# Identity and x loaded in parts, the angles' sine moved to chunk 7, and block A's last down product moved ahead of block B's last gate and up

## The reference, cut to what matters

```python
def first_block(x, ...):
    for l in range(DEPTH):                      # DEPTH = 2
        f = swiglu(rms_norm(x, ffn1_pre_g[l]), ffn1_w_gu[l], ffn1_w_down[l])
        x = x + 0.5 * rms_norm(f, ffn1_post_g[l])
        m = hybrid_mixer(rms_norm(x, mix_pre_g[l]), ...)
        x = x + rms_norm(m, mix_post_g[l])
        f = swiglu(rms_norm(x, ffn2_pre_g[l]), ffn2_w_gu[l], ffn2_w_down[l])
        x = x + 0.5 * rms_norm(f, ffn2_post_g[l])

def second_block(x, positions, ...):            # the same shape without the norms behind
    cos_r, sin_r = rope_tables(positions, 128); cos_m, sin_m = rope_tables(positions, 32)
    for l in range(DEPTH):
        x = x + 0.5 * swiglu_ffn(rms_norm_2(x, ffn1_norm[l]), ...)
        x = x + (retention and latent attention of rms_norm_2(x, mix_norm[l])) @ w_o[l]
        x = x + 0.5 * swiglu_ffn(rms_norm_2(x, ffn2_norm[l]), ...)
```

## Time and profile before

| | |
|---|---|
| Median of 3 runs | 2165.37 us (2163.66 to 2166.07) |
| Profiled execution | 2167.78 us, of which the span of the profile is 2166.5 us |
| TensorE busy | 1980.8 us, 91% of the span |
| VectorE, ScalarE, GpSimd busy | 1179.8, 1020.3 and 123.1 us |
| Mean granted TensorE clock | 0.967 of full speed |
| Share of the chain that ended last | PE 80%, DVE 9%, ACT 6%, issue 3%, POOL 3% |
| Data moved | 348.08 MB, mean 161 GB/s |

### The profile page before, as it was taken

How to read it: one execution, slowest core, us unless ns; L and a number is a source line. 1 busy time by engine, 2 the same in 40 slices (tenths; PEclk the granted TensorE clock), 3 DMA queues, 4 the chain that set the end, 5 groups by cost and what they waited for, 6 DMA issues and landing times.

```text
span 2166.5 us, 23846 instructions
## 1 busy us (share of the span) xinstructions
PE 1980.8 (91%) x9304; PEld 1645.9 (76%) x9304; DVE 1179.8 (54%) x1695; ACT 1020.3 (47%) x1675; POOL 123.1 (6%) x183
## 2 busy tenths in 40 slices
PE   2999887999899987999999996889999999688999
PEld 1888786888788786788778875778877887577887
DVE  2555666555655576555564455555555456555554
ACT  3444564444544475444454453544445444354443
POOL 4000021000000012000000012000000001200000
PEclk9999998999999997999999998999999999889999
DMA  4655323655555433455555542345545554233553
GB/s 150 209 189 191 117 98 126 206 191 196 173 191 198 149 127 118 139 192 194 174 174 198 178 134 97 117 133 191 198 158 182 192 175 137 95 117 128 193 193 108
DMA packets 95904, 348.08 MB, mean 161 GB/s; under 512 B 10800, under 2 KB 10800, under 8 KB 95408
## 3 DMA queue, kind: packets, MB, share of 16 engines
q1 hardware_dynamic: 94032, 339.57, 47.4%
q10 hardware_dynamic: 1728, 6.99, 0.9%
q0 software_dynamic: 32, 0.00, 0.0%
HBM read 345.47 MB, written 1.05 MB: 160 GB/s over the span
## 4 chain that ended last, share of the span: by engine, by line
PE 80%; DVE 9%; ACT 6%; issue 3%; POOL 3%; DMA 0%; ACTq 0%; POOLq 0%; DVEq 0%
PE ps_gu L362 16%; PE ps_gu L364 16%; PE ps_gu L363 16%; PE ps_acc L362 9%; PE ps_acc L363 9%; PE ps_acc L364 9%; DVE sb_wl L1184 4%; PE ps_tr L417 2%; ACT sb_wh L805 1%; POOL sb_scratch L1648 1%; ACT sb_xh L834 1%; PE ps_acc L381 1%; ACT sb_scratch L826 1%; DVE sb_scratch L1299 1%; PE ps_acc L542 0%
## 5 line engine op out<-in xcount | busy, mean ns | idle before, releaser
L1184 DVE TENSOR_TENSOR sb_wl<-sb_raw,sb_wh 128x1024 fp32r<-128x1024 f32 (+2 forms) x648 | 769.7, 1220 | 289.9 <-ACT sb_wh L805 281.8
L362 PE MATMUL ps_gu<-sb_wh,sb_xh 128*128 128x512 f32 (+2 forms) x1632 | 667.0, 409 | 93.4 <-DVE sb_xl L1231 43.9
L805 ACT ACTIVATE sb_wh<-sb_raw 128x1024 fp32r<-128x1024 f32 (+2 forms) x648 | 658.1, 1053 | 193.2 <-PE ps_acc L364 136.0
L364 PE MATMUL ps_gu<-sb_wh,sb_xl 128*128 128x512 f32 (+2 forms) x1632 | 645.4, 395 | 0.0
L363 PE MATMUL ps_gu<-sb_wl,sb_xh 128*128 128x512 f32 (+2 forms) x1632 | 644.1, 395 | 0.0
L362 PEld LDWEIGHTS ps_gu<-sb_wh,sb_xh 128*128 128x128 f32 x1632 | 313.4, 192 | 160.8 <-DVE sb_xl L1231 43.0
L364 PEld LDWEIGHTS ps_gu<-sb_wh,sb_xl 128*128 128x128 f32 x1632 | 313.1, 192 | 66.5
L363 PEld LDWEIGHTS ps_gu<-sb_wl,sb_xh 128*128 128x128 f32 x1632 | 314.8, 193 | 57.6
L362 PE MATMUL ps_acc<-sb_wh,sb_fr 128*128 128x512 f32 (+1 forms) x768 | 301.3, 392 | 8.9 <-DVE sb_fr L1269 8.9
L363 PE MATMUL ps_acc<-sb_wl,sb_fr 128*128 128x512 f32 (+1 forms) x768 | 299.7, 390 | 0.0
L364 PE MATMUL ps_acc<-sb_wh,sb_fr 128*128 128x512 f32 (+1 forms) x768 | 299.3, 390 | 0.0
(11 more groups left out here) (264 smaller groups left out, 1322.2 us busy)
## 6 DMA issues: line engine op xcount, KB each, us to landing
sb_raw<-stream SPq DMA_DIRECT2D x628, 512.0 KB, 4.5
sb_raw<-stream SPq DMA_DIRECT2D x8, 416.0 KB, 3.8
sb_raw<-stream SPq DMA_DIRECT2D x8, 390.0 KB, 3.7
sb_gpost<-post_gains ACTq DMA_DIRECT2D x6, 512.0 KB, 3.4
sb_params<-params ACTq DMA_DIRECT2D x2, 1128.5 KB, 5.8
sb_raw<-stream SPq DMA_DIRECT2D x4, 384.0 KB, 4.1
sb_x<-x SPq DMA_DIRECT2D x1, 1024.0 KB, 7.2
out<-sb_x SPq DMA_DIRECT2D x4, 256.0 KB, 2.2
```

Source lines behind the costliest of these rows:

```text
L362: pe.matmul(out, xh, wh, start=start, stop=False)
L364: return pe.matmul(out, xl, wh, start=False, stop=stop)
L805: go(m.wh[:, u % RING, 0:widths[u]], m.raw[:, u % RAW, 0:widths[u]], ACT.Copy).then_inc(*s.high_done.up())
L1184: tt(m.wl[:, u % RING, 0:w], m.raw[:, u % RAW, 0:w], m.wh[:, u % RING, 0:w].bitcast(F32), ALU.subtract).then_inc(*s.low_done.up())
```

## The change

1. The constants are loaded in two parts, the identity (128 columns) first, then the gains, then the rest. x is loaded by block, B's half behind the first two units of the stream. TensorE waits for the identity and block A's half, and for B's half at `turn_x(0, 1)`.
2. ScalarE and VectorE split one unit, then work on block A's x, then one unit, and then two. The sine and its negation move to the end of chunk 7 of stage 0. GpSimd's program keeps `angles()` as its first work.
3. In the last chunk of every feed-forward stage, the turn of A's hidden values and A's down product come directly behind B's down product of the chunk before, ahead of B's gate and up. The next stage's `turn_x(e, 0)` is placed within B's gate and up: behind its last quarter ahead of a mixer, behind its third quarter ahead of a feed-forward stage with a norm behind, and behind its second in the others. B's last turn and down product (`rest` on TensorE, called `finish` in the next stage) run in the middle of the next stage's A products, and `turn_x(e, 1)` comes behind those.
4. ScalarE and VectorE follow: two units of the next stage are split before the boundary; at the boundary `first` (B's silu or hidden values; two splits after a mixer) and `second` (the split of B's hidden values and two units; two splits after a mixer) stand at new places. For a feed-forward stage `first` comes behind `x_high` and `x_low` of block A, whatever stage went before.
5. The mean behind the sum is computed as soon as both squares are there, ahead of the second product with the gain. GpSimd's roots come in the order of the blocks.

```diff
             elif e:
                 pe.wait_ge(*s.x_ready[t].at(2 * (e - 1) + half + 1))
+            elif t:
+                pe.wait_ge(s.x_b_loaded, 16)
...
-    def ffn(f, e):
+    def ffn(f, e, finish):
...
-        turn_x(e, 0)
-        for j in range(CHUNKS):
-            if j == 0:
-                gate_up(j, 0, lambda: turn_x(e, 1), 2)
-            else:
+        last = CHUNKS - 1
+
+        def rest():
+            turn_hidden(last, 1)
+            down(last, 1)
+
+        if finish:
+            gate_up(0, 0, finish)
+            turn_x(e, 1)
+        else:
+            turn_x(e, 0)
+            gate_up(0, 0, lambda: turn_x(e, 1), 2)
+        for j in range(last):
+            if j:
                 gate_up(j, 0, lambda: turn_hidden(j - 1, 1))
                 down(j - 1, 1)
             gate_up(j, 1, lambda: turn_hidden(j, 0))
             down(j, 0)
-        turn_hidden(CHUNKS - 1, 1)
-        down(CHUNKS - 1, 1)
+        gate_up(last, 0, lambda: turn_hidden(last - 1, 1))
+        down(last - 1, 1)
+        turn_hidden(last, 0)
+        down(last, 0)
+        if e + 1 == len(STAGES):
+            gate_up(last, 1)
+        elif STAGES[e + 1][0] != "ffn":
+            gate_up(last, 1, lambda: turn_x(e + 1, 0), 3)
+        else:
+            gate_up(last, 1, lambda: turn_x(e + 1, 0), 2 if e + 1 <= POSTS else 1)
+        return rest
...
-        turn_x(e, 0)
-        chunk(e, 0, zdt, ZDT_W, m.gu[0][:, 0:ZDT_W], True, lambda: turn_x(e, 1), 2).then_inc(
-            *done("zdt0", l))
+        chunk(e, 0, zdt, ZDT_W, m.gu[0][:, 0:ZDT_W], True, finish).then_inc(*done("zdt0", l))
+        turn_x(e, 1)
...
-    pe.wait_ge(s.const_loaded, 16)
+    pe.wait_ge(s.ident_loaded, 16)
+    finish = None
     for e, (kind, n) in enumerate(STAGES):
-        {"ffn": ffn, "mix1": mix1, "mix2": mix2}[kind](n, e)
+        finish = {"ffn": ffn, "mix1": mix1, "mix2": mix2}[kind](n, e, finish)
+    finish()
...
+        post, mixer = 1 <= e <= POSTS, STAGES[e][0] != "ffn"
         for t in range(2):
             if post:
                 post_squares(e, t)
-            if t == 0:
-                between()
+            if e == 0 and t == 1:
+                act.wait_ge(s.x_b_loaded, 16)
             if mixer:
                 x_squares(e, t)
+            else:
                 x_high(e, t)
-            elif e < len(STAGES):
-                if t == 1:
-                    x_squares(e, 0)
+            if t == 0:
+                first()
+            if mixer:
                 x_high(e, t)
-                if t == 1:
-                    x_squares(e, 1)
+            else:
+                x_squares(e, t)
             if t == 0:
-                after()
+                second()
...
-        for j in range(CHUNKS):
+        last = CHUNKS - 1
+        for j in range(last):
             split(2)
             if j == 0:
                 load_ahead()
@@ -886,7 +912,21 @@
             hidden_high(j, 0)
             split(2)
             silu(j, 1)
-        return lambda: hidden_high(CHUNKS - 1, 1), lambda: None
+            if e == 0 and j == 7:
+                act.wait_ge(*s.angles.at(1))
+                for i in range(2):
+                    a = go(m.trig[:, i, :, :], m.trig[:, i, :, :], ACT.Sin)
+                a.then_inc(*s.trig.up())
+        split(2)
+        hidden_high(last - 1, 1)
+        silu(last, 0)
+        hidden_high(last, 0)
+        split(2)
+
+        def rest():
+            hidden_high(last, 1)
+            split(2)
+        return lambda: silu(last, 1), rest
...
-    act.dma_start(m.const[:, :], aps["const"]).then_inc(s.const_loaded, 16)
+    act.dma_start(m.const[:, 0:P], aps["const"][:, 0:P]).then_inc(s.ident_loaded, 16)
     act.dma_start(m.gpre[:, :, :], aps["pre_gains"]).then_inc(s.gains_loaded, 16)
+    act.dma_start(m.const[:, P:CONST_COLS], aps["const"][:, P:CONST_COLS]).then_inc(s.const_loaded, 16)
...
-    act.wait_ge(*s.angles.at(1))
-    for i in range(2):
-        a = go(m.trig[:, i, :, :], m.trig[:, i, :, :], ACT.Sin)
-    a.then_inc(*s.trig.up())
     act.wait_ge(s.x_loaded, 16)
     act.wait_ge(s.gains_loaded, 16)
-    split(4)
-    between = after = lambda: None
+    split(1)
+    first, second = lambda: split(1), lambda: split(2)
...
-    def update_post(e, t, between):
+    def update_post(e, t):
         vec.wait_ge(s.post_gain_loaded, 16 * e)
         post_scale(e, t, 0)
-        between()
-        post_scale(e, t, 1).then_inc(*s.post_scaled[t].up())
+        vec.wait_ge(*s.post_squared[t].at(2 * e))
         ts(m.pm[:, t:t + 1], m.pss[:, t, 0:1], m.pss[:, t, 1:2], EPS * (4 if HALF_STEP[e] else 1), ALU.add,
            ALU.add).then_inc(*s.post_mean[t].up())
+        post_scale(e, t, 1).then_inc(*s.post_scaled[t].up())
...
+        post, stage = 1 <= e <= POSTS, STAGES[e][0] if e < len(STAGES) else None
         for t in range(2):
-            first = between if t == 0 else nothing
             if post:
-                update_post(e, t, first)
+                update_post(e, t)
             elif e:
                 update(e, t)
-                first()
-            if mixer:
+            if stage == "ffn":
+                x_low(e, t)
+            elif stage:
                 x_mean(e, t)
                 normed(e, t)
+            if t == 0:
+                first()
+            if stage == "ffn":
+                x_mean(e, t)
+            elif stage:
                 x_low(e, t)
-            elif e < len(STAGES):
-                if t == 1:
-                    x_mean(e, 0)
-                x_low(e, t)
-                if t == 1:
-                    x_mean(e, 1)
             if t == 0:
-                after()
+                second()
...
+            if e == 0 and j == 7:
+                vec.wait_ge(*s.trig.at(1))
+                ts(m.trig[:, 2, :, :], m.trig[:, 1, :, :], -1.0, None, ALU.mult).then_inc(*s.trig.up())
+        split(2)
+        hidden_low(last - 1, 1)
+        hidden(last, 0)
+        hidden_low(last, 0)
+        split(2)
+
+        def rest():
+            hidden_low(last, 1)
+            split(2)
+        return lambda: hidden(last, 1), rest
...
-            if STAGES[e][0] != "ffn":
-                x_rms(e, t)
-            elif t == 1:
-                x_rms(e, 0)
-        if STAGES[e][0] == "ffn":
-            x_rms(e, 1)
+            x_rms(e, t)
...
-    sp.dma_start(m.x[:, :, :], aps["x"]).then_inc(s.x_loaded, 16)
+    sp.dma_start(m.x[:, 0, :], aps["x"][:, 0, :]).then_inc(s.x_loaded, 16)
     for u in range(UNITS):
+        if u == 2:
+            sp.dma_start(m.x[:, 1, :], aps["x"][:, 1, :]).then_inc(s.x_b_loaded, 16)
...
```

More of the change, by code:

```diff
@@ L491, in mix1 @@
         tile(1, tiles + 1, m.gu[1][:, 0:T])
+        pe.wait_ge(s.const_loaded, 16)
         pe.wait_ge(*V.at("ad", l))
@@ L609, in part @@
         def part(t, u0, name, width=512, first=False, midway=None):
-            p = chunk(e, t, u0, width, m.gu[t][:, 0:width], first, midway, 2)
+            p = chunk(e, t, u0, width, m.gu[t][:, 0:width], first, midway)
             p.then_inc(*done(f"{name}{t}", turn))
@@ L691, in retained @@
             p.then_inc(*done(f"y{t}", turn))
-        turn_x(e, 0)
-        part(0, lat, "lat", LAT_W, True, lambda: turn_x(e, 1))
+        part(0, lat, "lat", LAT_W, True, finish)
+        turn_x(e, 1)
         part(1, lat, "lat", LAT_W, True)
@@ L836, in x_high, with boundary @@
             a.then_inc(*s.x_high[t].up())
-    def boundary(e, between, after):
-        post, mixer = 1 <= e <= POSTS, e < len(STAGES) and STAGES[e][0] != "ffn"
+    def boundary(e, first, second):
+        post, mixer = 1 <= e <= POSTS, STAGES[e][0] != "ffn"
         for t in range(2):
@@ L1147, in mix2 @@
         return lambda: split(2), lambda: split(2)
-    act.dma_start(m.const[:, :], aps["const"]).then_inc(s.const_loaded, 16)
+    act.dma_start(m.const[:, 0:P], aps["const"][:, 0:P]).then_inc(s.ident_loaded, 16)
     act.dma_start(m.gpre[:, :, :], aps["pre_gains"]).then_inc(s.gains_loaded, 16)
+    act.dma_start(m.const[:, P:CONST_COLS], aps["const"][:, P:CONST_COLS]).then_inc(s.const_loaded, 16)
     table(SILU)
-    act.wait_ge(*s.angles.at(1))
-    for i in range(2):
-        a = go(m.trig[:, i, :, :], m.trig[:, i, :, :], ACT.Sin)
-    a.then_inc(*s.trig.up())
     act.wait_ge(s.x_loaded, 16)
     act.wait_ge(s.gains_loaded, 16)
-    split(4)
-    between = after = lambda: None
+    split(1)
+    first, second = lambda: split(1), lambda: split(2)
     for e, (kind, n) in enumerate(STAGES):
-        boundary(e, between, after)
-        between, after = {"ffn": ffn, "mix1": mix1, "mix2": mix2}[kind](n, e)
-        assert at_unit[0] == min(FIRST_UNIT[e + 1] + 4 * (kind == "ffn"), UNITS), (e, kind, at_unit[0])
-    between()
+        boundary(e, first, second)
+        first, second = {"ffn": ffn, "mix1": mix1, "mix2": mix2}[kind](n, e)
+        assert at_unit[0] == min(FIRST_UNIT[e + 1] + 2 * (kind == "ffn"), UNITS), (e, kind, at_unit[0])
+    first()
+    second()
 def vector_program(nc, m, s, m1, m2):
```

(15 more changed lines are left out.)

9 lines of the change are left out of this document (5 added, 4 removed).

## The result

The changed kernel takes 2187.47 us (median of 4 runs, 2184.18 to 2189.09), the kernel before 2165.72 beside it (4 runs, 2163.66 to 2168.34): ratio 1.0098, 95% interval 1.008 to 1.0115, so slower by 17 to 25 us. I had forecast slower, at 2172.9 and not above 2182. The profiled execution took 2189.09 us (span 2187.5, for 2166.5 before), and TensorE's mean granted clock was 0.956 for 0.967.

What follows compares the result with a forecast made beforehand. TensorE works 91% of the span, so only its waits at the start and eleven boundaries count: -11.7 + 11.2 + 3.8 - 3.4 + 2.0 + 3.2 + 2.4 = +7.5, 2172.9 us by the median; 8-in-10 range 2161 to 2182.

Steps and rivals of the forecast that it cites:

- The start: Stage 0: turn of A's hidden values at 40.5 for 53.70, less 1.5 for a slow stretch; gain 11.7, bounds 9.5 to 17.6.
- Rival 3: Start: the angles aren't on the path, so the start follows the first product, 29 us earlier; 2155.6, chance 0.06.
- The clock: Boundaries: slow stretches cost 2.1 each at stages 1, 4 and 1.1 each at 7, 10; -3.2 at 3, 6, 9; sum +3.2.
- stages 1 and 4: Feed-forward to mixer: B's first product after 27.5 us for 29.2, -1.7 each, before the clock's 2.1 each.
- stages 8 and 11: Feed-forward after a mixer, no norm behind: splits behind x_high delay B's turn, +2.7 or +3.7 each, 3.2 taken.
- The waits: Boundaries and end: longer or shorter idle time of TensorE from the new order, forecast apart from the slow-clock terms.
- -3.2 for slow stretches of the old order: Two of stages 3, 6, 9: a slow-clock stretch lay on the path and no longer does, -3.2.
- Stages 2 and 5: Feed-forward after a mixer, norm behind: splits wait behind x_high, B's turn at 11.4 for 9.03, +2.4 each.
- stages 7 and 10: Feed-forward to mixer: B's first product at 25.5 for 23.6, +1.9 each, before the clock's 1.1 each.
- the three between feed-forward stages: Stages 3, 6, 9: one hand-off more, A's wait shorter, B's longer; +0.7 each, +2.0 together, between 0 and +3.5.
- Rival 5: Whole kernel: every unknown at its dear end, 11 more than forecast, 2184, slower; chance 0.07.
- Rival 1: Boundaries: the clock stays up and no new slow stretch falls on the path; 2165.5, no change; chance 0.14.

Runs made afterwards that it cites:

- E1: The kernel before with only the new start (loads in parts, one split ahead of A's first products, sine in chunk 7), boundaries as before: 2154.98 us.
- E2: E1 with stage 0's two inverse roots ahead of the angles on GpSimd: 2137.6 us.
- E3: The changed kernel with stage 0's two inverse roots ahead of the angles on GpSimd: 2167.0 us.
- E5: The changed kernel with TensorE's waits at the boundaries and the end filled by transposes that nobody reads: 2170.98 us.
- E7: The changed kernel with GpSimd's masking of gate weights in stages 1 and 4 held until B's normed values are made: 2184.22 us.
- E6: E2, with the old boundaries, plus unread transposes ahead of each block's first products at the boundaries: 2132.81 us.
- E8: The changed kernel with roots ahead of the angles, two splits ahead of x_high behind a mixer, masking later and waits filled with transposes: 2142.23 us.
- E10: E6 with GpSimd's masking behind block B's normed values, nothing added in the second mixer: 2132.36 us.

## Why the prediction was wrong in size

- **The start** was right: -11.7 forecast, -11.6 in the trace. In part that is luck. The constants came 1.6 later than forecast and the angles were stretched 1.5 less. And the slow stretch behind the wait cost the 1.5 forecast here, but 2.8 in E1, which turned A's hidden values 0.2 later and gained 10.0. Rival 3 needed the roots ahead of the angles; E2 and E3 made it come true.
- **The clock** is the step that failed. I priced the slow stretches that the new order puts on the path at 7.4 (2.1 each at stages 1 and 4, 1.1 each at 7 and 10, 0.5 each at 8 and 11, none at the end). E5 takes most of them away, and between its trace and that of the change they are 17.6: 3.5 and 6.0 at stages 1 and 4, 2.3 and 2.2 at 8 and 11, 0.9 and 2.4 at 7 and 10, 1.6 at the end, about -1 in the others together. That is 10.2 of the 13.4 us by which the boundaries missed. I had priced a slow stretch at up to 1.5, as it cost behind 2 to 3 us of idle time, and kept that price behind 4.2. There 18 products took 2.8 longer, and at stages 8 and 11, where products end last and the clock had stayed up before, most of it was lost. Why stages 1 and 4 lost most isn't settled: B's turn there was slow before too, and E7's trace loses 3.4 less at stage 4 than the change's.
- **The waits** were near in most stages and short in sum. Without the 7.4 the prediction's boundaries and end come to 11.8, which holds the -3.2 for slow stretches of the old order that no longer lie on the path. E5 has 15.0 there (+3.3 at the end of its trace, -11.7 in stage 0), with 5.24 for 5.1 in front of the first product: 3.2 more. Stages 2 and 5 gave 2.2 and 2.6 for 2.4, stages 8 and 11 4.0 and 3.1 for 2.7 (1.4 of the 4.0 is a slow stretch in the output products ahead of the turn, which the change has too), stages 7 and 10 2.2 and 0.3 for 1.9, and the three between feed-forward stages +1.0 together for 2.0 - 3.2 = -1.2.
- **A second count** sets E5 beside E6, where the old order has transposes too, and not beside the kernel before. E5 takes 38.2 us more, of which the roots are 17.4 (E1 less E2), so the new order costs 20.8 with the clock held, for 15.0 forecast without any clock term. The rest of the 32.5 that the boundaries cost by medians is the clock, 11.7 for 4.2. The boundaries between feed-forward stages cost 1.3, 1.3 and 1.7 in these traces for my 0.7 each: I had let the silu chain hide part of a hand-off that is paid in full. By this count the waits are short by some 6 us and the clock by 7 to 8; it stays the larger part of the miss.
- **Overlooked:** GpSimd's masking beside B's normed values, 1.05 at stages 1 and 4. It lay on the path of before as well; I built B's new time from A's chain, which it doesn't touch.
- **Rival 5**, every unknown at its dear end, gave 2184 and was nearest, but for another reason: the stretches between feed-forward stages were cheap (-0.8, +0.8, -1.2 with the clock) and the slow ones dearer than its dear end. Rival 1 is what E5 made: a clock that stays up. It had 2165.5, 7.4 less than forecast; E5 has 2171, 5.5 above it, 3.2 of it the waits above.
- **Left open:** how the 10 us of E8 divide. In the traces E8 and E10 lie 13.9 apart behind stage 0: 4.4 at stages 3, 6 and 9, 4.3 at 7 and 10, 2.5 at the end, and 2.7 at the other six. The hand-offs of 1.3 us that nothing covers explain the first and the last in kind; no run took one away. Why the constants land 2.0 later is not tested either: the load now stands third on ScalarE's queue.

## What to carry over

Price an idle stretch of TensorE by what it does to the work behind it: where the wait gets longer and products end last behind it, they can be worth as much as the wait itself, here 17.6 us of 32.6. A reorder that closes one engine's gap moves every other engine's queue too; what had been done early in a mixer's shadow (the two splits) must stay there. And look for a producer that sits in program order behind a long chain of no urgency (the roots behind the angles): moving it took a few lines and gave 17 to 20 us, more than the rest of the new start (10 to 12).

## What the hardware did that was not expected

- Transposes of the identity, 0.115 us each and read by nobody, kept TensorE's granted clock at 1.00 behind a wait of 4.2 us of which they filled all but 1.15 (E5, stage 2); without them it was 0.50 for the next 6 us.
- A VectorE operation with one SBUF input, the 128x512 scaling, is also held up by GpSimd: 1.93 for 0.88 the pair, in the change and not in E7. In the prediction I had looked only at the other direction. The Trainium skill, GPSIMD Engine Reference, Specifications, names a 2-port mode of VectorE's instructions beside two inputs as a cause of such contention. The trace would agree if the scaling ran in that mode, which no row shows.
- GpSimd's operation that meets a split took 0.7 to 0.9 more, not a whole split of 1.2, and of six splits five met one: the first was over before the angles began.
